# Linear attention in a two-block network: decay factors by products of neighbouring blocks and a scan, in place of logs, cumulative matmuls and exponentials

## The reference

```python
def gla_chunked(q, k, v, log_a, s0, with_output):
    """Chunked GLA: S_t = diag(a_t) S_{t-1} + k_t v_t^T, o_t = q_t S_t."""
    def step(S, inp):
        qc, kc, vc, ac = inp
        b = jnp.cumsum(ac, axis=2)
        bC = b[:, :, -1:, :]
        S_new = jnp.exp(bC[:, :, 0, :, None]) * S + jnp.einsum(
            'bhjd,bhjv->bhdv', kc * jnp.exp(bC - b), vc)
        if not with_output:
            return S_new, None
        diff = b[:, :, :, None, :] - b[:, :, None, :, :]
        decay = jnp.exp(jnp.where(tri[:, :, None], diff, -jnp.inf))
        scores = jnp.einsum('bhid,bhjd,bhijd->bhij', qc, kc, decay)
        o = jnp.einsum('bhij,bhjv->bhiv', scores, vc) + jnp.einsum(
            'bhid,bhdv->bhiv', qc * jnp.exp(b), S)
        return S_new, o

def gla_bidir(q, k, v, la_f, la_b, s0_f, s0_b, with_output):
    o_f, s_f = gla_chunked(q, k, v, la_f, s0_f, with_output)
    o_b, s_b = gla_chunked(flip(q), flip(k), flip(v), flip(la_b), s0_b, with_output)
    return (o_f + flip(o_b) if with_output else None), s_f, s_b

def gla_log_decay(lowrank, w_up, b):
    gk = (lowrank @ w_up + b).astype(jnp.float32)
    return (jax.nn.log_sigmoid(gk) / GATE_NORM).reshape(B, L, GLA_HEADS, GLA_DK)
```

## Time and profile before

| | us |
|---|---|
| median of 3 runs | 3113.21 (3106.71 to 3122.37) |
| the profiled execution, its time | 3106.99 |
| its span, first to last instruction | 3105.2 |
| P, 334 to 722 | 388 |
| S, 722 to 860 | 138 |
| F, 860 to 1136 | 276 |

### The profile page before, as it was taken

How to read it: one execution, slowest core, us unless ns; L and a number is a source line. 1 busy time by engine, 2 the same in 40 slices (tenths; PEclk the granted TensorE clock), 3 DMA queues, 4 the chain that set the end, 5 groups by cost and what they waited for, 6 DMA issues and landing times.

```text
span 3105.2 us, 36143 instructions
## 1 busy us (share of the span) xinstructions
PE 2773.8 (89%) x12500; PEld 2180.5 (70%) x12500; DVE 1410.6 (45%) x2057; ACT 744.3 (24%) x1109; POOL 947.5 (31%) x449
## 2 busy tenths in 40 slices
PE   2899999999968768999669998999879999999997
PEld 1688777778757655777358676667747777777775
DVE  7774122221157757651339434544143544444446
ACT  2311233331023225320231123544031110001102
POOL 1243333333213342443025230000223443334444
PEclk8899999999979888999879996988989999999999
DMA  7465444445454433222201011212201111111111
GB/s 264 161 226 190 165 170 169 169 156 194 171 186 139 166 131 140 81 88 96 80 27 41 27 33 55 62 53 61 88 27 41 48 42 48 47 47 47 41 47 68
DMA packets 124934, 317.77 MB, mean 102 GB/s; under 512 B 11584, under 2 KB 42880, under 8 KB 124224
## 3 DMA queue, kind: packets, MB, share of 16 engines
q1 hardware_dynamic: 72576, 197.31, 19.0%
q10 hardware_dynamic: 52288, 119.52, 10.7%
HBM read 243.77 MB, written 73.01 MB: 102 GB/s over the span
## 4 chain that ended last, share of the span: by engine, by line
PE 50%; issue 5%; DVE 5%; ACT 1%; DMA 1%; DVEq 0%; ACTq 0%
PE pb L432 39%; PE g L2199 3%; PE g L2165 2%; PE g L469 2%; PE g L2181 1%; PE pb L2167 1%; PE g L2056 1%; DMA x<-xp_d 1%; DVE zcs L1622 0%; PE g L2147 0%; DVE x L1872 0%; DVE hl L1813 0%; PE g L2096 0%; DVE xin L1331 0%; ACT ptr L1148 0%
## 5 line engine op out<-in xcount | busy, mean ns | idle before, releaser
L631 POOL TENSOR_TENSOR w_hi<-w_raw,one 128x1024 fp32r<-128x1024 f32 x177 | 349.8, 1976 | 1929.0 <-PE pb L432 1896.9
L432 PE MATMUL pb<-xh,w_hi 128*128 128x512 f32 (+1 forms) x1400 | 545.0, 389 | 69.1 <-DVE xl L1327 68.2
L432 PE MATMUL pb<-xh,w_lo 128*128 128x512 f32 (+1 forms) x1400 | 537.7, 384 | 0.0
L432 PE MATMUL pb<-xl,w_hi 128*128 128x512 f32 (+1 forms) x1400 | 537.7, 384 | 0.0
L634 POOL TENSOR_TENSOR w_lo<-w_raw,w_hi 128x1024 fp32r<-128x1024 f32 x177 | 477.0, 2695 | 13.9
L432 PEld LDWEIGHTS pb<-xh,w_hi 128*128 128x128 f32 x1400 | 265.3, 189 | 135.8 <-issue 81.0
L432 PE MATMUL pb<-mh,w_hi 128*128 128x512 f32 x832 | 334.1, 402 | 27.9 <-DVE ml L1327 23.0
L432 PE MATMUL pb<-mh,w_lo 128*128 128x512 f32 x832 | 332.5, 400 | 0.0
L432 PE MATMUL pb<-ml,w_hi 128*128 128x512 f32 x832 | 332.1, 399 | 0.0
L432 PEld LDWEIGHTS pb<-xl,w_hi 128*128 128x128 f32 x1400 | 265.5, 190 | 57.4
L432 PEld LDWEIGHTS pb<-xh,w_lo 128*128 128x128 f32 x1400 | 266.2, 190 | 55.1 <-issue 0.5
(11 more groups left out here) (270 smaller groups left out, 4279.0 us busy)
## 6 DMA issues: line engine op xcount, KB each, us to landing
w_raw<-in_wall SPq DMA_DIRECT2D x177, 512.0 KB, 3.5
mod_raw<-in_modw SPq DMA_DIRECT2D x72, 512.0 KB, 5.6
proj_d<-stage ACTq DMA_DIRECT2D x44, 512.0 KB, 2.7
at_bias<-in_bias SPq DMA_DIRECT2D x64, 256.0 KB, 2.6
proj_d<-stage ACTq DMA_DIRECT2D x13, 640.0 KB, 3.4
fla<-la_d SPq DMA_DIRECT2D x8, 1024.0 KB, 5.5
svt<-vt_d ACTq DMA_DIRECT2D x12, 512.0 KB, 4.4
vc<-proj_d ACTq DMA_DIRECT2D x10, 512.0 KB, 4.6
```

Source lines behind the costliest of these rows:

```text
L432: mm = pe.matmul(pb[bank][:, 0:n], w[:, b, wc:wc + P], x[:, k, tokens], start=(count == 0), stop=(count == total - 1))
L631: nc.gpsimd.tensor_tensor(w_hi[:, b, :], w_raw[:, b, :], one[:, 0:1].to_broadcast([P, 1024]), ALU.mult).then_inc(w_high, 1)
```

## The change

Decays are no longer kept as logs. P: the gate product comes out with channels on the partitions, in eight products of 128 tokens (stationary `wup_sb`); Abs, Exp, Ln and the subtraction stay, then a second Exp gives the decay factors `av` themselves (scale 1/16). A scan on VectorE, `run = run * av + reset`, backwards over 516 elements and once for each direction, gives the running products, set to one at the start of each head; `kd` is the key times it, and eight transposes of `kd` after the second tile give `kt`, which ScalarE copies. The totals `dec` are columns of `run`. Queries are loaded, rotated and stored in P too (`qc`, `qs`, `qr_d`), and the keys are rotated in place, so that the loads into them stand after the first tile's store and wait for the stores of the chunk before. Only the eight chunks of `x` have queries.

F: SyncE loads rotated queries and keys and the factors `fa`. `f_first` multiplies the queries by their own factor. `f_grow(c, l)` makes level l + 1 of queries and keys from level l: `lq` and `lk` outside the border, `bq` and `bk` inside it, and the products `span` of neighbouring blocks; ScalarE copies the halves that need no further factor (`f_kept`). Scores use four PSUM banks instead of two. The loops over chunks are written out.

```diff
@@ SyncE
             def f_load(c, b):
+                sp.dma_start(fq[:, b].rearrange("p h n -> p (h n)"), qr_d[c]).then_inc(f_in[b], 16)
+                for d in range(2):
+                    sp.dma_start(fa[:, b, d].rearrange("p (h n) -> p h n", n=CH),
+                                 a_d[c].rearrange("p (a h n) -> a p h n", a=2, n=CH + 1)[d][:, :, d:d + CH])\
+                      .then_inc(f_in[b], 16)
                 sp.dma_start(fk[:, b].rearrange("p h n -> p (h n)"), kr_d[c]).then_inc(f_in[b], 16)
-                sp.dma_start(fq[:, b], rows_of(T_Q, 4)[:, :, c, :]).then_inc(f_in[b], 16)
-                load_swapped(sp, fs[:, b], rows_of(T_Q, 4)[:, :, c, :], f_in[b])
-                sp.dma_start(fla[:, b].bitcast(F32).rearrange("p a d n -> p a (d n)"),
-                             la_d[c].rearrange("a p n -> p a n")).then_inc(f_in[b], 16)
...
@@ ScalarE, P
             def p_load(c, b, queries):
...
+                if queries:
+                    act.dma_start(qc[:, b], rows_of(T_Q, 4)[:, :, c, :]).then_inc(p_in[b], 16)
+                    load_swapped(act, qs[:, b], rows_of(T_Q, 4)[:, :, c, :], p_in[b])
...
-                if more:
+                p_tile(i, 3 * b)
+                if after is not None:
                     act.wait_ge(p_kt, c + 1)
-                    p_load(i * 2 + (b + 1), 1 - b)
-                p_tile(i, 3 * b)
+                    act.wait_ge(p_out[1 - b], i * 80 + (80 + 80 * b))
+                    p_load(i * 2 + (b + 1), 1 - b, after)
                 act.wait_ge(p_gk, c + 1)
...
-                act.wait_ge(p_la, c + 1)
-                act.activation(lah[:, b], la[:, :, :], ACT.Copy).then_inc(p_lah, 1)
+                act.wait_ge(p_la, c + 2)
+                for d in range(2):
+                    act.activation(av[:, b, d, :, d:d + CH],
+                                   soft[:, d, :].rearrange("p (h n) -> p h n", n=CH), ACT.Exp,
+                                   scale=1.0 / GATE_NORM).then_inc(p_av, 1)
...
@@ ScalarE, F
-                        act.activation(ex[:, n % 2, h, :], g[:, h, :], ACT.Exp).then_inc(f_exp, 1)
+            def f_kept(c, l):
+                b, m = c % 2, 1 << l
+                act.wait_ge(f_rec, REC * c + 2 if l == 0 else rec(c, l - 1, 4))
+                act.activation(inner(lq[:, l + 1], m), inner(bq[:, :, :], m), ACT.Copy).then_inc(f_cpy, 1)
...
@@ VectorE, P
-                nc.vector.tensor_tensor(lal[:, b], la[:, :, :], lah[:, b], ALU.subtract).then_inc(p_lal, 1)
-                nc.vector.tensor_tensor(kt[:, b, 0, :], ef[:, 0, :], g[:, 2, :], ALU.mult)
-                nc.vector.tensor_tensor(kt[:, b, 1, :], ef[:, 1, :], g[:, 2, :], ALU.mult).then_inc(p_kt, 1)
+                for d in range(2):
+                    dve.wait_ge(p_av, i * 4 + (2 * b + d + 1))
+                    step_, last = (-1, H + HEADS - 1) if d == 0 else (1, 0)
+                    backward = [view(x, last, (step_, H + HEADS)) for x in (run[:, d], av[:, b, d])]
+                    nc.vector.tensor_tensor_scan(
+                        backward[0], backward[1], view(reset[:, :, :], 0, (1, H + HEADS)), 0.0,
+                        ALU.mult, ALU.add).then_inc(p_run, 1)
+                for d in range(2):
+                    dve.wait_ge(p_run, i * 4 + (2 * b + d + 1))
+                    v = nc.vector.tensor_tensor(kd[:, d], kc[:, b], run[:, d, :, 1 - d:1 - d + CH], ALU.mult)
+                v.then_inc(p_kd, 1)
@@ VectorE, F
+            def f_grow(c, l):
...
+                nc.vector.tensor_tensor(outer(lq[:, l + 1], m), outer(lq[:, l], m), factor(s + 1, 1 - s),
+                                        ALU.mult).then_inc(f_rec, 1)
+                nc.vector.tensor_tensor(outer(lk[:, l], m), outer(lkl, m), factor(1, s + 1),
+                                        ALU.mult).then_inc(f_rec, 1)
+                nc.vector.tensor_tensor(span[l + 1][:, :, :], view(t, 0, (s, 2), (2, s // 2)),
+                                        view(t, 1, (s, 2), (2, s // 2)), ALU.mult).then_inc(f_rec, 1)
+                dve.wait_ge(f_cpy, CPY * c + 2 * l + 1)
+                nc.vector.tensor_tensor(inner2(bq[:, :, :], m), inner2(lq[:, l], m), factor(0, s + 3),
+                                        ALU.mult).then_inc(f_rec, 1)
+                if l < LEVELS - 2:
+                    dve.wait_ge(f_cpy, CPY * c + 2 * l + 2)
+                    nc.vector.tensor_tensor(inner2(bk[:, :, :], m), inner2(lkl, m), factor(s, 3 - s),
+                                            ALU.mult).then_inc(f_rec, 1)
...
+            for c in range(NCX):
+                f_first(c)
+                for l in range(4):
+                    f_grow(c, l)
+                if c:
+                    f_update(c - 1)
+                f_choose(c, 0)
+                f_grow(c, 4)
+                f_choose(c, 1)
+                f_grow(c, 5)
+                f_choose(c, 2)
+                f_last(c)
+                for l in range(3, LEVELS):
+                    f_choose(c, l)
@@ TensorE, P
-                for h in range(HEADS):
-                    mm = pe.transpose(g[:, 2, CH * h:CH * h + CH], kr[:, b, h, :], ident)
-                mm.then_inc(p_ktr, 1)
                 p_tile(i, 3 * b + 1)
-                pe.wait_ge(p_lal, c + 1)
-                for d in range(2):
-                    for n, x in enumerate((lah, lal)):
-                        pe.matmul(g[:, d, :], matr[:, d, :], x[:, b, d, :], start=(n == 0), stop=(n == 1))
+                pe.wait_ge(p_kd, c + 1)
+                pe.wait_ge(p_kt, c + 1)
+                for d in range(2):
+                    for h in range(HEADS):
+                        mm = pe.transpose(g[:, 2 + 3 * d, CH * h:CH * h + CH], kd[:, d, h, :], ident)
+                mm.then_inc(p_ktr, 1)
                 p_tile(i, 3 * b + 2)
```

406 lines of the change are left out of this document (195 added, 211 removed).

## The result

The changed kernel took 3173.2 us (median of four runs, 3152.3 to 3186.5) beside 3117.8 for the kernel before; the ratio is 1.0176, with an interval of 1.0106 to 1.0246. A second measurement, six runs on another occasion, gave 3162.4 us and 1.0164 (1.0137 to 1.0191). The direction was predicted, the size was not: 3131 was given, with a range up to 3155.

What follows compares the result with a forecast made beforehand. It took TensorE's stream to bound P, and a chain of waits with two level loops to decide F. +49 and -29 made +20 on 3106.99 us: 3127, 3133 by the runs' median; 3131 was given, range 3098 to 3155.

Steps and rivals of the forecast that it cites:

- P, +49: Stage P (decays and keys of each chunk): TensorE stands still for the decayed keys behind ScalarE's loads, +49 us in all.
- the clock: In P, after each long stall, TensorE's clock stays at 1.2 GHz for a time: 2.5 us lost a chunk.
- F, -29: Stage F (outputs of each chunk): shorter first chunk and turns, less GpSimd's waits for VectorE, -29 us in all.
- the second turn: In F, SyncE's second turn starts at 895.5 instead of 915.15 (-19.6 us); the turn itself gains 3.1.
- waits that vanish (-6.6): In F, SyncE's waits in a turn for the end of a chunk go: some 6.6 us over six turns.
- a third turn of -3.1: In F, a turn carries 0.75 of 3.5 MB less, so GpSimd begins 11.3 us in instead of 14.4: -3.1 us.
- four turns of +2.0: In F from the fourth turn, VectorE's products hold GpSimd until 16.4 us into the turn: +2.0 us for four turns.
- the ring: In F, SyncE's turn of chunk load and pooling tile halves waiting for GpSimd, which VectorE's 7.9 us of products hold.
- (a): Rival, level: GpSimd slips between VectorE's products (F -45), the clock falls late in P's stalls (+38): 3106 us, chance 0.27.
- (b): Rival, faster: P's issues overlap with the wait or cost 0.33 us each, P +10, F -45: 3078 us, chance 0.12.
- (c): Rival, slower still: TensorE's gaps in F leave it at 1.2 GHz, F -8, P +49: 3154 us, chance 0.11.

Runs made afterwards that it cites:

- e3: Changed kernel, VectorE in F waiting before each level's products for the last operation of the level below: 3145.5 us, ratio 1.010 to the kernel before.
- later start: VectorE's first keys' copy before the second block's attention split in five: changed kernel 3153.8 and 3153.2 us, kernel with both edits 3031.7 and 3044.2 us.
- e2: Changed kernel, SyncE in F issuing each pooling tile's first two transfers ahead of the next chunk's load: 3117.6 us, ratio 0.998 to the kernel before.
- e4: Changed kernel, F's pooling tiles taken out of the turns and done behind the last chunk: 3248.9 us (one run).

## Why the prediction was wrong, point by point

**P, +49, was +42 with its start.** The mechanism and its terms held: thirteen issues of 0.53 us between the store and Abs (predicted 0.52), a wait of 5.45 us (5.7) at the second tile's end, scans of 1.21 to 1.23 us (1.23), a chunk of 44.5 us (45.8). The term that was mis-sized is the clock: 2.5 us a chunk were given, from a return five microseconds after the work resumed. It fell 2.2 us into the wait (494.1) and came back 3.5 us after its end (500.9), within the eight transposes and the four or five products behind them, about 1.8 us lost. The Trainium skill ("DVE: opcode table, instruction layouts, handler registers and perf-mode slots", Datapath and trigger behaviour) had the scan at half throughput; the trace agrees, 1.22 us for 516 elements against 0.68 for the two-input operation of 512 beside it.

**F, -29, was -4.** This step failed. Against the earlier trace rows, the second turn starts 15.4 us earlier instead of 19.6, the second itself gains 1.8 instead of 3.1, and the last gains 4.5 instead of 4.3. The failure is in the sum of the turns between: predicted were waits that vanish (-6.6), a third turn of -3.1 and four turns of +2.0; measured were five turns of +3.1, +1.4, +4.5, +4.3 and +4.0. GpSimd was held from the third turn on, not the fourth; the burst began 9.2 us into the turn instead of 8.5, and it lasted 9.0 us instead of 7.9, because the products of level 0, which read `fa`, start 0.55 us apart and not the 0.34 taken from the earlier trace rows, and the two 512-element ones 0.72 to 0.75 apart. GpSimd's first operation so ended as one that begins 18.2 us into the turn and not 16.4. The prediction had the right place for the ring and took its length from the wrong row.

**The rule of the Trainium skill that was weighed there** ("GPSIMD Engine Reference", Key points: the interfaces are shared, with contention when VectorE has two SBUF inputs) is borne out: the held operation ends its own length after the first VectorE operation with an input in PSUM, and gaps in the burst (e3) halve it. Beside the `zcs` operations GpSimd mostly got in all the same, so two SBUF inputs alone do not say how long it is held.

**Behind F, 0, was +42 in the profiled run.** That unchanged code keeps its time was assumed and stood in no step. It is the larger part of the miss in that run: the attention stage took 345 us instead of 303, with the clock at 0.71 instead of 0.82. In the medians, 55 and 45 us, the stages up to F hold 38.6 by these profiles, and 7 to 17 us are left for all that stands behind. The later start's 7 to 15 us fit that, but the stretch from F to that stage differs as much between profiles (728 to 750 us), so how the rest divides is open.

**The rivals.** (a) needed GpSimd to slip between VectorE's products; it did not. (b) needed issues that overlap with the wait or cost 0.33 us each; they took 0.53 each, in full. (c) gave 3154 with F at -8, the nearest of the sums, but by TensorE's clock in F; that clock did fall (0.74 against 0.87), beside a VectorE that was waiting for its load, so it cost little: e2 shortened F by 43 us with the clock at 0.79, and e3 by 24 with the clock at 0.72. That it came nearest is luck.

Its arithmetic is not what made the change slower. With ScalarE's loads left where they were and the pooling tile's first transfers put ahead, it makes the kernel 2.0 to 2.3% faster than the one before, and with the later start about 2.4 to 2.5% (ratio 0.9746, interval 0.9679 to 0.9813, and 0.9763, interval 0.9743 to 0.9783).

## What to carry to other kernels

Count the DMA issues that stand between a producer and the activation that reads it: each held ScalarE for half a microsecond, and moving them by one statement was worth 53 us. When one loop of two gets faster, look at what the faster engine now does while the other works: a burst of two-input VectorE operations that used to have gaps held GpSimd for its whole length, and the order of four transfers, or a wait, gave the time back. And compare two kernels stage by stage with the clock beside it, before a difference is put down to the code that was changed: a third of a microsecond in front of a stage in which the clock rises and falls moved 14 to 42 us in the profiles and 7 to 15 in the means of the runs.

## What the runs showed of the chip that was not expected

In F GpSimd got no turn at all between VectorE's two-input products (0.2 to 0.8 us each) that followed each other without a gap: 8.6 us for an operation of 1.06, and a pause of 0.03 us let it in. Beside operations of 1.27 us in an equally close row it mostly got in behind the running one, and in 6 of 20 profiles it was held for 27.6 us. A VectorE product of 256 elements starts 0.55 us after the last in level 0 and 0.34 in the levels above, also where GpSimd is idle (e4). In level 0 its elements of `fa` lie alternately at two distant places; that this is the reason was not tested, and one of 512 elements that reads every second one of `fa` took 0.60 us, as long as one that reads them side by side. TensorE's clock can fall in a stage where it is busy over 90% of the time, and stages with equal code took 303, 317, 330, 340 or 345 us, the same few lengths again and again: 303 to 317 where the clock first came back within 52.1 us of the stage's start, 330 to 345 where it came 0.3 us later. At 1.2 GHz TensorE was busy 96 to 98% of that stage.
